# Two-block sequence model on one core: last eight gate units and third branch product of each layer from rounded weight parts, S5 demodulation over two banks at once

## The reference, cut to what matters

```python
z = n @ w_in                      # 1024 -> 5808, split into q/k/v parts, SSM input, 3 * 1024 gate columns
o_mla = mla_mixer(...)            # attention, 512 wide
o_gla = gla_mixer(...)            # gated linear attention, 512 wide
o_s5  = s5_mixer(...)             # complex diagonal state space, 512 wide, ends in a GLU
gates = sigmoid(gate_in + gate_b) # three gates of 1024
mixed = g0 * (o_mla @ w_br_mla) + g1 * (o_gla @ w_br_gla) + g2 * (o_s5 @ w_br_s5)
x = x + mixed @ w_out
x = x + relu(norm(x) @ w_ff1)**2 @ w_ff2
```

## Time and profile before

| | |
|---|---|
| median of three timed runs | 2425.92 us (2425.4 to 2427.27) |
| the profiled execution, its own time | 2425.09 us |
| its span in the trace | 2423.3 us, mean granted clock of TensorE 0.925 |
| TensorE matmuls busy | 2070.2 us, 85% of the span |
| VectorE busy | 1053.2 us, 43% |
| ScalarE busy | 715.4 us, 30% |
| DMA | 625.50 MB, mean 258 GB/s |

### The profile page before, as it was taken

How to read it: one execution, slowest core, us unless ns; L and a number is a source line. 1 busy time by engine, 2 the same in 40 slices (tenths; PEclk the granted TensorE clock), 3 DMA queues, 4 the chain that set the end, 5 groups by cost and what they waited for, 6 DMA issues and landing times.

```text
span 2423.3 us, 30772 instructions
## 1 busy us (share of the span) xinstructions
PE 2070.2 (85%) x12383; PEld 1500.8 (62%) x12383; DVE 1053.2 (43%) x2134; ACT 715.4 (30%) x1178; POOL 29.0 (1%) x49
## 2 busy tenths in 40 slices
PE   7999999776667676666666899989999999899999
PEld 5987789533333333333333576768988867679887
DVE  3987766300001111101001256763775457755854
ACT  3547853100000000000000123642554325623542
POOL 0000000000000000000000200000000200000000
PEclk8999999888887878888888999989999999899999
DMA  9545754999999999999999843304445425123552
GB/s 349 174 148 209 209 173 160 403 419 420 419 419 420 419 420 420 419 419 420 419 420 420 322 125 118 122 35 174 173 175 190 136 80 191 70 105 139 187 195 87
DMA packets 173697, 625.50 MB, mean 258 GB/s; under 512 B 9760, under 2 KB 28736, under 8 KB 125168
## 3 DMA queue, kind: packets, MB, share of 16 engines
q1 hardware_dynamic: 172144, 622.19, 66.3%
q0 software_dynamic: 1408, 1.29, 0.3%
HBM read 628.69 MB, written 1.05 MB: 260 GB/s over the span
## 4 chain that ended last, share of the span: by engine, by line
PE 58%; DMA 20%; SPq 11%; DVE 6%; ACT 4%; issue 2%; POOL 0%; DVEq 0%; POOLq 0%; ACTq 0%
PE pb L178 21%; DMA ring<-in_w 12%; SPq L1140 10%; PE pb L363 9%; DMA ar<-in_w 5%; PE pb L364 4%; PE pb L1224 4%; PE pb L1250 2%; DMA ring<-in_w_in 1%; PE pb L579 1%; PE pb L581 1%; PE pb L580 1%; PE pb L457 1%; PE pb L459 1%; PE pb L458 1%
## 5 line engine op out<-in xcount | busy, mean ns | idle before, releaser
L178 PE MATMUL pb<-ar,ring 128*128 128x256 f32 x2400 | 544.0, 385 | 9.5 <-ACT ar L2164 6.7
L178 PEld LDWEIGHTS pb<-ar,ring 128*128 128x128 f32 x2400 | 453.4, 191 | 88.7 <-issue 12.4
L363 PE MATMUL pb<-act,parts 128*128 128x512 f32 x944 | 337.5, 399 | 0.0
L1224 PE MATMUL pb<-ring,ar 128*32 128x512 f32 x1448 | 244.2, 688 | 85.2 <-DMA ring<-in_w 61.7
L364 PE MATMUL pb<-act,parts 128*128 128x256 f32 x944 | 264.5, 280 | 0.0
L1250 PE MATMUL pb<-ring,ar 128*32 128x512 f32 x704 | 151.7, 857 | 74.5 <-DMA ring<-in_w 57.2
L363 PEld LDWEIGHTS pb<-act,parts 128*128 128x128 f32 x944 | 177.5, 188 | 39.8
L2082 DVE TENSOR_TENSOR parts<-ring,parts 128x2048 fp32r<-128x2048 f32 x72 | 161.7, 2287 | 85.6 <-ACT parts L2075 85.6
L1224 PEld LDWEIGHTS pb<-ring,ar 128*32 128x32 f32 x1448 | 63.2, 124 | 209.1 <-issue 208.4
L1453 DVE TENSOR_TENSOR ar<-ar,pb 128x512 f32<-128x512 f32 x16 | 11.0, 688 | 412.7 <-PE pb L1224 412.7
L364 PEld LDWEIGHTS pb<-act,parts 128*128 128x128 f32 x944 | 178.2, 189 | 3.4
(11 more groups left out here) (419 smaller groups left out, 3087.3 us busy)
## 6 DMA issues: line engine op xcount, KB each, us to landing
ring<-in_w SPq DMA_DIRECT2D x269, 1024.0 KB, 26.8
ar<-in_w SPq DMA_DIRECT2D x115, 1024.0 KB, 26.7
ring<-in_w_in SPq DMA_DIRECT2D x36, 2048.0 KB, 9.0
ring<-in_w_ff SPq DMA_DIRECT2D x32, 2048.0 KB, 7.9
ring<-in_w_ada SPq DMA_DIRECT2D x12, 2048.0 KB, 14.5
ring<-in_w_ssm_out SPq DMA_DIRECT2D x4, 2048.0 KB, 8.9
ring<-in_w_out SPq DMA_DIRECT2D x4, 2048.0 KB, 7.7
ring<-in_w_cv_out SPq DMA_DIRECT2D x2, 2048.0 KB, 7.8
```

Of the source, the lines that this page charges most:

```text
L178: ins = e.matmul(out, l, r, start=(i == 0), stop=(i == len(pairs) - 1))
L363: e.matmul(p, wh, both, start=first, stop=False)
L1224: ins = e.matmul(k.pb[b][32 * j:32 * j + 32, :], v.xg[i][:, kt, 32 * j:32 * j + 32], w[j][:, m, :], start=(kt == 0), stop=(kt == 7))
```

## The change

- Gate units 16 to 23 and branch 2 are computed with three float32r matmuls per K tile in place of one float32 matmul. The weight blocks (gates 16 to 19, gates 20 to 23, `w_br_s5`) are split by `cut_high` (ScalarE) and `cut_low` (VectorE); the remainder is written in place of the raw weights. The activations `n` and `oc` are split too (`gate_high`, `gate_low`, `oc_high`, `oc_low`).
- ScalarE's order in the tail becomes: cut 0, eight copies of `n`, cut 1, four copies of `oc`, cut 2, sigmoids of gates 16 to 23, `ff_high` of block 0, `mg_high`. VectorE's becomes: cut 0, eight `gate_low`, branch 1, cut 1, four `oc_low`, cut 2, `ff_low` of block 0, branch 2 with `mg_low`.
- SyncE loads `w_br_s5` into slot 3 where block 0 of `w_out` was, and blocks 0 and 1 of `w_out` into slots 0 and 1 when the gate units that read them are through.
- `demodulate` reads both banks in four 512-wide operations; both banks are freed together.

```diff
@@ layer_sp
-    slots.load(e, "raw", 3, [128, 8, 512], ff_source(a, l, 0), ("ff_low", 2 * (NSPLIT * l + 1)))
+    branch(2, 3)
     columns("gate16", 0)
     columns("gate20", 1)
-    branch(2, 2)
-    for j in range(1, NSPLIT):
-        if j < 3:
-            e.wait_ge(*k.at(*slots.free[j % 2]))
+    for j in range(NSPLIT):
+        if j < 2:
+            e.wait_ge(*k.at(*slots.free[j]))
@@ new
+CUTS = [("gate16", 0, 4, [8, 512]), ("gate20", 1, 5, [8, 512]), ("w_br_s5_2", 3, 2, [4, 1024])]
+def cut_high(k, o, l, b):
+    name, raw, high, shape = CUTS[b]
+    i, count = k.held[l, name]
+    o.e.wait_ge(*k.at(f"layer_slot{i}", count))
+    if b < 2:
+        o.e.wait_ge(*k.at("ob", 2 * l + 2))
+    else:
+        o.e.wait_ge(*k.at("mm_branch", 24 * l + 16))
+    s = shape[0] // 2
+    for half in range(2):
+        o.done(o.e.activation(as_parts(k, high, shape)[:, s * half:s * half + s, :], k.slot(raw, ...)[:, ...], ACT.Copy), k.s("cut_high"))
+def cut_low(k, o, l, b):
+    for half in range(2):
+        o.e.wait_ge(*k.at("cut_high", 6 * l + 2 * b + half + 1))
+        o.done(o.e.tensor_tensor(as_parts(k, raw, shape)[:, rows, :], ..., ..., ALU.subtract), k.s("cut_low"))
@@ layer_pe, a gate unit from gate16 on (branch 2 the same with four K tiles)
+                for j in range(8):
+                    e.wait_ge(*k.at("cut_low", 6 * l + 2 * cut + j // 4 + 1))
+                    e.wait_ge(*k.at("gate_low", 8 * l + j + 1))
+                    e.matmul(k.pb[b][:, 0:T], wh[:, j, c], v.gate_high[j], start=(j == 0), stop=False)
+                    e.matmul(k.pb[b][:, 0:T], wl[:, j, c], v.gate_high[j], start=False, stop=False)
+                    ins = e.matmul(k.pb[b][:, 0:T], wh[:, j, c], v.gate_low[:, j, :], start=False, stop=(j == 7))
@@ ff_high
     elif j == 1:
-        o.e.wait_ge(*k.at("ff_low", 2 * (NSPLIT * l + 1)))
         o.e.wait_ge(*k.at("mm_branch", 24 * l + 24))
+    else:
         o.e.wait_ge(*k.at("mm_unit", NUNIT * (l + 1)))
-    else:
-        o.e.wait_ge(*k.at("ob", 2 * l + 2))
-        o.e.wait_ge(*k.at("oc", l + 1))
@@ layer_ac
+    cut_high(k, o, l, 0)
+    e.wait_ge(*k.at("mm_out", 8 * l + 8))
+    for m in range(8):
+        if m == 7:
+            e.wait_ge(*k.at("oc", l + 1))
+        o.done(e.activation(v.gate_high[m], v.n[:, m, :], ACT.Copy), k.s("gate_high"))
+    cut_high(k, o, l, 1)
+    for m in range(4):
+        o.done(e.activation(v.oc_high[:, m, :], v.oc[:, m, :], ACT.Copy), k.s("oc_high"))
+    cut_high(k, o, l, 2)
+    units.upto("gate23")
     ff_high(k, o, l, 0)
-    units.upto("gate23")
@@ layer_ve, demodulate
-        for q in range(2):
-            b = k.pb[k.bank["s5_in", 16 * l + 2 * u + q]]
-            ...
+        vr, vi = k.pair[:, :, 0:256], k.pair[:, :, 256:512]
+        o.done(e.tensor_tensor(v.pr, vr, c, ALU.mult))
+        t1 = o.done(e.tensor_tensor(v.sx, vi, s, ALU.mult))
+        o.done(e.tensor_tensor(v.pi, vi, c, ALU.mult))
+        t2 = o.done(e.tensor_tensor(v.sy, vr, s, ALU.mult), k.s("demodulated"))
@@ layer_ve, tail
+    cut_low(k, o, l, 0)
+    after_unit(k, e, l, "gate15")
+    for m in range(8):
+        e.wait_ge(*k.at("gate_high", 8 * l + m + 1))
+        o.done(e.tensor_tensor(v.gate_low[:, m, :], v.n[:, m, :], v.gate_high[m].bitcast(F32), ALU.subtract), k.s("gate_low"))
+    for m in range(8):
+        branch(1, m)
+    cut_low(k, o, l, 1)
+    for m in range(4):
+        ...
+    cut_low(k, o, l, 2)
+    units.upto("gate23")
     ff_low(k, o, l, 0)
-    for br in (1, 2):
-        for m in range(8):
-            branch(br, m)
-            if br == 2 and m:
-                mg_low(m - 1)
-        if br == 1:
-            units.upto("gate23")
+    for m in range(8):
+        branch(2, m)
+        if m:
+            mg_low(m - 1)
```

More of the change, by code:

```diff
@@ L117, in __init__ @@
         self.sems = {}
-        self.pb = [ctx.enter_context(nc.psum_tensor(f"pb{i}", [128, 512], F32)) for i in range(8)]
+        single = [ctx.enter_context(nc.psum_tensor(f"pb{i}", [128, 512], F32)) for i in range(2)]
+        self.pair = ctx.enter_context(nc.psum_tensor("pb2", [128, 2, 512], F32))
+        self.pb = single + [self.pair[:, i, :] for i in range(2)] + [ctx.enter_context(nc.psum_tensor(f"pb{i}", [128, 512], F32)) for i in range(4, 8)]
         self.h = self.sb("h", [128, NK, T])
@@ L1622, in __init__ @@
         self.nh, self.nl = k.act[:, 8:16, :], k.act[:, 16:24, :]
+        self.gate_high = [k.act[:, 79 - m, :] for m in range(8)]
+        self.gate_low, self.oc_high, self.oc_low = k.act[:, 0:8, :], k.act[:, 33:37, :], k.act[:, 16:20, :]
         self.high = [k.act[:, 24 + m, :] for m in range(32)]
@@ L1635, in unit_place, with as_parts @@
     return {"kpe0": v.kpe[:, 0, :], "kpe1": v.kpe[:, 1, :], "gv0": v.gv[:, 0, :], "gv1": v.gv[:, 1, :], "lr": v.lr[0:16, :]}[name], None
+CUTS = [("gate16", 0, 4, [8, 512]), ("gate20", 1, 5, [8, 512]), ("w_br_s5_2", 3, 2, [4, 1024])]
+def as_parts(k, i, shape):
+    x = k.raw[:, i, :] if i < 2 else k.parts[:, i - 2, :]
+    return x.rearrange("p (k n) -> p k n", k=shape[0])
+def cut_high(k, o, l, b):
[8 more added lines that the diff above has]
+    for half in range(2):
+        o.done(o.e.activation(as_parts(k, high, shape)[:, s * half:s * half + s, :], k.slot(raw, [128] + shape)[:, s * half:s * half + s, :], ACT.Copy), k.s("cut_high"))
+def cut_low(k, o, l, b):
+    name, raw, high, shape = CUTS[b]
+    s = shape[0] // 2
+    for half in range(2):
+        rows = slice(s * half, s * half + s)
+        o.e.wait_ge(*k.at("cut_high", 6 * l + 2 * b + half + 1))
+        o.done(o.e.tensor_tensor(as_parts(k, raw, shape)[:, rows, :], k.slot(raw, [128] + shape)[:, rows, :], as_parts(k, high, shape)[:, rows, :].bitcast(F32), ALU.subtract), k.s("cut_low"))
 BRANCHES = (("w_br_mla_2", 0), ("w_br_gla_2", 1), ("w_br_s5_2", 2))
@@ L1928, in inputs @@
         both = [s5_ring.take(("s5_in", 16 * l + 2 * u + q)) for q in range(2)]
+        both = sorted(both)
         for i in range(2):
@@ L1933, in inputs @@
         for q in range(2):
-            s5_ring.until(both[q], *k.at("demodulated", 16 * l + 2 * u + q + 1))
+            s5_ring.until(both[q], *k.at("demodulated", 8 * l + u + 1))
         ins.then_inc(k.s("mm_in"), 1)
@@ L1964, in branch @@
         name, x = BRANCHES[br][0], (v.oa, v.ob, v.oc)[br]
-        w, at = landed(name, [128, 4, 1024]), 24 * l + 8 * br + m
+        w, at = None if br == 2 else landed(name, [128, 4, 1024]), 24 * l + 8 * br + m
         e.wait_ge(*k.at(("oa", "ob", "oc")[br], (4 * l + 4, 2 * l + 2, l + 1)[br]))
         b = ring.take(("branch", at))
+        if br == 2:
+            wl, wh = (as_parts(k, s, CUTS[2][3]) for s in CUTS[2][1:3])
+            c = slice(128 * m, 128 * m + 128)
+            for i in range(4):
+                e.wait_ge(*k.at("cut_low", 6 * l + 4 + i // 2 + 1))
+                e.wait_ge(*k.at("oc_low", 4 * l + i + 1))
+                e.matmul(k.pb[b][:, 0:T], wh[:, i, c], v.oc_high[:, i, :], start=(i == 0), stop=False)
+                e.matmul(k.pb[b][:, 0:T], wl[:, i, c], v.oc_high[:, i, :], start=False, stop=False)
+                ins = e.matmul(k.pb[b][:, 0:T], wh[:, i, c], v.oc_low[:, i, :], start=False, stop=(i == 3))
+            ins.then_inc(k.s("mm_branch"), 1)
+            ring.until(b, *k.at("branch", at + 1))
+            return
         k.group(e, k.pb[b][:, 0:T], [(w[:, i, 128 * m:128 * m + 128], x[:, i, :]) for i in range(4)]).then_inc(k.s("mm_branch"), 1)
@@ L2053, in ff_raw @@
 def ff_raw(k, e, l, j):
[L2055 to L2059, removed]
+    e.wait_ge(*k.at(f"ff_raw{j % 2}", 16 * (9 * l + j // 2 + 1)))
     return k.slot(j % 2, [128, 8, 512])
```

20 lines of the change are left out of this document (11 added, 9 removed).

## The result

| | before | after |
|---|---|---|
| median of 10 runs, us | 2426.49 | 2433.26 |
| lowest to highest | 2425.05 to 2429.59 | 2429.91 to 2434.25 |
| profiled execution: own time, span | 2425.09, 2423.3 | 2433.7, 2431.9 |

The change makes the kernel slower: ratio 1.0025, 95% interval 1.0017 to 1.0034, which is 6.1 us, or 6.8 us by the medians. I forecast 2435.6, with a range of 2428 to 2443.

A forecast was written before the change was run, and what follows sets the result against it. TensorE alone was taken to bound the tail. Products -6.8, wait +7.6 or +6.2, clock +2.5, tail end +3.0, demodulation -0.75 give +5.55 and +4.15, together +9.7 us: 2434.8, as median 2435.6, range 2428 to 2443.

The forecast's parts named there:

- the wait: TensorE stands before branch 1's eighth product until VectorE first reads branch 1: +7.6 us first layer, +6.2 us second.
- a load alone: Bound for the first gate block's load: 7.7 us by itself, which gives a first-layer TensorE wait of 5.5 us.
- Products: Gates 16 to 23 and branch 2 in the tail: three split products replace one float32 matmul, -6.8 us a layer.
- The second wait in front of each K tile: Added waits before the tail's K tiles: taken as free, at most 0.05 us each, 5 us a layer.
- the medians of the pairs: Durations of the two gate block loads, 11.0 and 10.2 us, used to put the first block at 9.8 and 8.4.
- The path behind the landing: From the first gate block's landing through split, eight gate_low and first branch 1 read: 9.6 us.
- The Trainium skill's fit: About 2 us plus bytes over 436 GB/s: gate block lands in 6.8 us, both TensorE waits 4.6 us each.
- The clock: Behind the wait before branch 1's eighth product, TensorE's lower clock costs +2.5 us a layer, between 1.7 and 4.3.
- End of the tail: Split of w_out block 0 waits for the last gate, delaying branch 2 and h_mid: +3.0 us a layer, bounds 0 and 6.4.
- Demodulation: Four 512-wide operations replace eight on VectorE, little of it on the path: -0.75 us a layer, bounds 0 and -3.0.
- Rival 1: Second clock drop while TensorE waits for single mg_low: another 1.7 us a layer, 2439 us; chance 0.14.
- Rival 3: Cut 0 and gate_low done before TensorE reaches branch 1's eighth product, savings stand: -9.1 us, 2416.8 us; chance 0.08.

The follow-up runs named there:

- front_order: Changed kernel with ScalarE's gate_high copies ahead of cut 0, and VectorE's gate_low and five branch 1 reads ahead of cut 0's subtraction; 2417.86 us, 0.9970 of before.
- fill_stall: Changed kernel plus twelve float32 matmuls, results never read, in TensorE's wait ahead of branch 1's eighth product; 2430.53 us, 1.0014 of before.
- parts_only: Changed kernel with the old 256-wide demodulation put back, so the split parts alone; 2434.22 us, 1.0040 of before.
- both_again: Repetition of both_orders, run beside both_old_demod on the same chip; 2411.29 us, 0.9934 of before.
- end_order: Changed kernel with the halves of w_out's block 0 exchanged, so its high part needs only gate 19, not the last gate; 2427.59 us, 1.0008 of before.
- both_old_demod: Changed kernel with the reorderings of front_order and end_order, but the old 256-wide demodulation; 2413.89 us, 0.9953 of before.
- demod_only: Kernel before with the 512-wide demodulation alone; 2424.68 us, 0.9995 of before.
- both_orders: Changed kernel with the reorderings of front_order and end_order together; 2411.09 us, 0.9940 of before.

## Why the prediction was right

The sign and the places were right; the sum was 2.9 us too high (+9.7 against +6.8 by the medians, or +6.1 in the two profiles without their first row). One term, the wait, holds nearly all of that; with a load alone taken for it the same sum would have been +6.9, and that this meets the medians to 0.1 us is luck, as the weave alone scatters by more.

1. **Products, -6.8 a layer: right.** A gate unit takes 2.88 us, and with both losses ordered away the tail is 6.4 us shorter, 0.4 of the difference being the first square's wait. The second wait in front of each K tile, charged at nothing, shows nothing: the steady starts are 0.12 us apart.
2. **The wait, +7.6 and +6.2: this term was mis-sized.** It measured 5.3 and 5.7. The step that failed is "The last byte of both blocks has moved at about 1650.1 in the first layer", and with it "the medians of the pairs then put the first block at 9.8 and 8.4 us". I took the fall of the traffic for its end. In the kernel before 27 GB/s still moved in 1650 to 1651, and the next microsecond is not empty either:

```profile
1651.00:1652.00 1.00, 1.00 (x7) 0.87 (x6) 0.97 (x3) 0.00 (x0) 0.00 (x0) 1.00 0.03 12
```

The trace of the kernel before has the landings themselves, issue by issue: 7.9 and 14.2 us after the two issues in the first layer, 7.8 and 12.7 in the second. In the kernel after they are 7.8 and 14.0, and 8.1 and 13.1. So the medians of the pairs were right; my share of them between the two blocks was not. The path behind the landing was right: 9.60 us against about 9.6. The value 7.7 of a load alone, which I kept as a bound, was the better choice: it gave 5.5. `front_order` shows that the wait is nothing but this order.

3. **The Trainium skill's fit** (SBUF — State Buffer, the DMA setup-cost knee) gave an estimated 6.8 us for 2 MB; 7.77 and 8.13 were measured. The trace does not agree exactly: it is 1.0 and 1.3 us longer. The waits of 4.6 us worked out from the page's figure were too short by 0.7 and 1.1; mine were too long by 2.3 and 0.5.
4. **The clock, +2.5 a layer: right**, 2.62 and 2.46 against `fill_stall`. It is not a constant: in `parts_only`, with the same wait of 5.3 us, the same stretch is 2.1 and 2.0 us longer than in `fill_stall`. The stretches add up: the kernel after against `both_again` is 5.50 + 2.69 + 2.32 us longer in the first tail and 5.86 + 2.54 + 2.31 in the second, and less the 6.4 us of item 1 that makes the +4.1 and +4.3 of the table above.
5. **End of the tail, +3.0 a layer: right.** VectorE started branch 2's reads at 1690.36 and ended the last `mg_low` at 1699.72, and the first `w_out` product ended at 1700.2; without the three waits and what follows them it would have ended at 1697.8, 2.4 us sooner. The third stretch gives 2.3, and with the square's 0.4 it is 2.7. `end_order` takes the 2.3 away in both layers, and in `front_order` it stands alone.
6. **Demodulation, -0.75 a layer: right in sign, its size is not settled.** Four operations take 2.41 us, as forecast. TensorE's waits fall by 0.4 in two places, which is the forecast; the weaves of the two profiles give -1.2 a layer, those of all ten -0.9, `both_old_demod` 2.6 us for both layers in medians, `demod_only` 1.2 by its ratio. All lie between the bounds of 0 and -3.0 a layer.
7. **Rival 1, a second clock drop**, did not come: in the kernel after the granted clock is 1.00 from 1696 to 1706, where TensorE waits for `mg_low`, and its matmuls there keep starting 0.12 us apart. **Rival 3, faster**, asked for a wait of some 3 us or less. The waits were 2.3 and 2.7 us longer than that, but the mechanism exists: where `front_order` takes the wait away, the kernel is faster by 0.30%.

## What to carry to other kernels

Cheaper instructions on a full engine pay only if what feeds them doesn't move into its way. Here 13.6 us of savings were real, and two places where an in-order engine did late work (a load's split, a block's split) ahead of early work (reads that free banks) cost 21 us. When you add work to an engine that has room, ask for each operation behind it who waits for that, and put work on data still in flight behind reads whose data is ready. An idle time of the bounding engine also costs what its clock loses afterwards: here 2.0 to 2.7 us on top of 5.2 to 5.7.

## What the runs showed of the hardware

- The end of a load is set by its slowest part. In the kernel after the traffic of the second 2 MB block falls from 354 to 31 GB/s at 1651.0, but 20 GB/s at a DMA share of 0.06, one in sixteen, go on until past 1652.0; the last packet is at 1652.53, and the load lands at 1652.97. In the second layer it is 2170.40 and 2170.84. Read off the fall of the traffic, the first of these landings is 2 us too early; behind the last packet it comes 0.4 us later.
- Two such loads issued within half a microsecond are served one after the other, not side by side: in the first layer of the kernel after they landed 7.8 and 14.0 us after their issues, the first at the time of a load alone (7.7), when 2.39 of the 4.2 MB had begun to move. Over the two layers of all ten profiles the first of the pair landed 7.7 to 8.1 us after its issue, but for three cases: 9.1 (`demod_only`, first layer), 9.1 (`fill_stall`, second layer) and 9.3 (`both_orders`, second layer); the second of the pair landed after 12.7 to 14.3 us. Each load has sixteen packets of 4 bytes, and it lands 0.4 to 0.6 us after the last of them. In the three late cases fifteen of them come in time and the sixteenth 1.3 to 1.6 us behind; of the second blocks sixteen in twenty have such a straggler (1.1 to 1.6 us), and these are the ones that take 13.9 to 14.3 us. `both_orders`, second layer, from 2153.5 to 2154.5 and from 2154.5 to 2156.5:

```profile
DMA packets 195, 0.37 MB, mean 369 GB/s; under 512 B 15, under 2 KB 15, under 8 KB 195
DMA packets 377, 0.77 MB, mean 385 GB/s; under 512 B 1, under 2 KB 1, under 8 KB 377
```

That each of these packets closes the part of one DMA engine is my reading; why one part is late I don't know.
- The weave, with the same instructions and the same waits, was 222.9 to 228.8 us long in different executions, while tails and feed-forward repeat to 0.1 us in most. It is the stretch with many short waits, in which the granted clock moves between its two levels. The clock goes with the length at the ends of this range: its mean is 0.98 over the weave of 222.9 us (`demod_only`, first layer) and 0.95 over those of 228.3 (the same execution, second layer) and 228.8 us (`fill_stall`, second layer), with TensorE's waits adding up to the same within 0.5 us. Why it falls more often in one execution than in another was not tried.
